# A third group of seven products per pair in the retention's output product

## What is computed

```python
    y = ((y - mu) * lax.rsqrt(var + GN_EPS)).astype(x.dtype)
    y = y.transpose(0, 2, 1, 3).reshape(B, S, H * dv)
    gate = jax.nn.silu(jnp.einsum('bsd,de->bse', x, w_g))
    return jnp.einsum('bse,ed->bsd', gate * y, w_o)
...
        h = layer_norm(DEEPNORM_ALPHA * h + m, ln_g[i, 0], ln_b[i, 0])
```

## Time and profile before

| | |
|---|---|
| median of 3 runs | 2553.68 us (2552.9 to 2553.84) |
| the profiled execution, its own time | 2553.18 us |
| its span, first to last instruction | 2551.4 us |
| PE busy | 2536.5 us (99%) |
| DVE busy | 1809.2 us (71%) |
| ACT busy | 1275.8 us (50%) |
| retention's output product in it | 1655.8 to 1828.6 us |

### The profile page before, as it was taken

How to read it: one execution, slowest core, us unless ns; L and a number is a source line. 1 busy time by engine, 2 the same in 40 slices (tenths; PEclk the granted TensorE clock), 3 DMA queues, 4 the chain that set the end, 5 groups by cost and what they waited for, 6 DMA issues and landing times.

```text
span 2551.4 us, 39946 instructions
## 1 busy us (share of the span) xinstructions
PE 2536.5 (99%) x14214; PEld 2213.2 (87%) x14214; DVE 1809.2 (71%) x2040; ACT 1275.8 (50%) x1427; POOL 15.9 (1%) x39
## 2 busy tenths in 40 slices
PE   9999999999999999999999999999999999999998
PEld 8999888888888888888888888888888888888887
DVE  6666667767676789965655555587866766678997
ACT  4444444555555555534444444454455555555553
POOL 0000000000000000000000000000000000000000
PEclk9999999999999999999999999999999999999999
DMA  8554584555555556655555555546455555556564
GB/s 282 178 172 160 184 256 141 198 196 191 197 192 195 199 212 233 224 176 180 181 176 180 184 179 180 190 182 251 161 191 188 197 197 194 192 198 214 196 228 153
DMA packets 142036, 496.08 MB, mean 194 GB/s; under 512 B 15616, under 2 KB 17920, under 8 KB 141952
## 3 DMA queue, kind: packets, MB, share of 16 engines
q1 hardware_dynamic: 131616, 474.93, 54.2%
q10 hardware_dynamic: 10336, 20.03, 2.5%
HBM read 492.80 MB, written 2.10 MB: 194 GB/s over the span
## 4 chain that ended last, share of the span: by engine, by line
PE 98%; DVE 1%; DMA 1%; issue 0%; ACT 0%; POOL 0%; DVEq 0%; ACTq 0%; SPq 0%; POOLq 0%
PE acc_cm L556 12%; PE acc_ab L556 11%; PE acc_ab L456 9%; PE acc_ab L453 9%; PE acc_ab L455 9%; PE acc_cm L559 6%; PE acc_ab L559 6%; PE acc_ab L467 4%; PE acc_ab L469 4%; PE acc_ab L470 4%; PE acc_cm L453 3%; PE acc_cm L455 3%; PE acc_cm L456 3%; PE acc_cm L725 1%; PE acc_cm L727 1%; PE acc_cm L726 1%
## 5 line engine op out<-in xcount | busy, mean ns | idle before, releaser
L1182 DVE TENSOR_TENSOR w_lo<-raw,w_hi 128x1024 fp32r<-128x1024 f32 x814 | 984.1, 1222 | 536.6 <-ACT w_hi L850 533.1
L850 ACT ACTIVATE w_hi<-raw 128x1024 fp32r<-128x1024 f32 (+1 forms) x818 | 850.6, 1053 | 614.3 <-PE acc_ab L456 181.5
L556 PE MATMUL acc_cm<-x_parts,w_hi 128*128 128x512 f32 x1408 | 480.1, 389 | 0.0
L556 PE MATMUL acc_ab<-x_parts,w_hi 128*128 128x512 f32 x1280 | 436.2, 389 | 0.0
L559 PE MATMUL acc_cm<-x_parts,w_lo 128*128 128x256 f32 x1408 | 388.6, 276 | 0.0
L559 PE MATMUL acc_ab<-x_parts,w_lo 128*128 128x256 f32 x1280 | 353.3, 276 | 0.0
L556 PEld LDWEIGHTS acc_cm<-x_parts,w_hi 128*128 128x128 f32 x1408 | 264.3, 188 | 54.6
L467 PE MATMUL acc_ab<-x_parts,w_hi 128*128 128x256 f32 x1020 | 284.5, 279 | 2.2 <-DVE x_parts L1211 0.9
L556 PEld LDWEIGHTS acc_ab<-x_parts,w_hi 128*128 128x128 f32 x1280 | 240.3, 188 | 49.7
L470 PE MATMUL acc_ab<-x_parts,w_lo 128*128 128x256 f32 x1020 | 281.9, 276 | 0.0
L469 PE MATMUL acc_ab<-x_parts,w_hi 128*128 128x256 f32 x1020 | 281.8, 276 | 0.0
(11 more groups left out here) (214 smaller groups left out, 3618.7 us busy)
## 6 DMA issues: line engine op xcount, KB each, us to landing
raw<-in_weights_dram SPq DMA_DIRECT2D x818, 512.0 KB, 3.8
unit_raw<-in_weights_dram SPq DMA_DIRECT2D x80, 512.0 KB, 8.4
next_raw<-in_weights_dram ACTq DMA_DIRECT2D x12, 512.0 KB, 4.3
ln_gain<-in_ln_g_dram ACTq DMA_DIRECT2D x16, 256.0 KB, 5.4
ln_bias<-in_ln_b_dram ACTq DMA_DIRECT2D x16, 256.0 KB, 7.0
h<-in_x_dram ACTq DMA_DIRECT2D x4, 512.0 KB, 7.7
x_t<-in_x_by_feature_dram SPq DMA_DIRECT2D x7, 256.0 KB, 7.7
raw<-in_weights_dram SPq DMA_DIRECT2D x4, 256.0 KB, 4.7
```

The source lines that it names most:

```text
L556: pe.matmul(acc[:, f], wh[:, k, c], x_parts[:, CK * s + k].rearrange("p a n -> p (a n)"), start=s == 0 and k == 0, stop=False, skip_group_ ...
L850: return act.activation(o, i, ACT.Copy)
L1182: dve.tensor_tensor(wl, raw[:, at % RING], wh.bitcast(F32), ALU.subtract).then_inc(lo_ready, 1)
```

## The change

Stage 1 takes three groups per pair, for heads 0 to 2. Head 2's sums are made in the retention loop as those of heads 0 and 1 are: its pass is written out and the loop over the other heads gets one pass shorter, on ACT and DVE. Six chunks per block are then in groups and ten are plain. So that the number of items is a multiple of four, chunk 11 of the second block is given as two items of one 128-row half each (`HALVED`); a pair has 42 items, the stage 84. The groups stand at items 10, 21, 32, 45, 56 and 66. With three groups per pair the buffers alternate within a pair (`buffer_of`: 0, 1, 0), and a semaphore's count is no longer half the group's number (`unit_use`). The norm's parameters are loaded behind the last group that uses buffer 0 (`SIDE_FREE`): from slot 73, where it was slot 48.

```diff
-UNITS = [4, 2, 4]
+UNITS = [4, 3, 4]
...
-LEAD = [[[12, 16, 20, 24], [4, 8, 12, 16]], [[11, 15], [3, 12]], [[12, 16, 20, 24], [3, 7, 11, 15]]]
-PAIR = [2 * (INNER[g] - 2 * UNITS[g]) + ITEMS * UNITS[g] for g in range(3)]
+LEAD = [[[12, 16, 20, 24], [4, 8, 12, 16]], [[10, 14, 18], [3, 7, 10]], [[12, 16, 20, 24], [3, 7, 11, 15]]]
+
+WHOLE, HALVES = slice(0, CK), [slice(k, k + 1) for k in range(CK)]
+HALVED = [[], [(1, 11)], []]
+PLAIN = [[(b, chunk, part) for b in range(2) for chunk in range(2 * UNITS[g], INNER[g])
+          for part in (HALVES if (b, chunk) in HALVED[g] else [WHOLE])] for g in range(3)]
+PAIR = [len(PLAIN[g]) + ITEMS * UNITS[g] for g in range(3)]
...
+def buffer_of(g, v):
+
+    return v % UNITS[g] % 2
+
+
+def unit_use(g, v):
+
+    return 1 + sum(buffer_of(a, b) == buffer_of(g, v) for a in range(g + 1) for b in range(v if a == g else 2 * UNITS[a]))
...
-              [UNIT_AFTER[g][1] + 5 + s for s in range(RING)] for g in range(3)]
+              [UNIT_AFTER[g][1] + 4 + s for s in range(RING)] for g in range(3)]
+SIDE_FREE = [max(at + ITEMS for v, at in enumerate(UNIT_AT[g]) if buffer_of(g, v) == 0) for g in range(3)]
...
-                            sp.wait_ge(lo_ready, base + unit_at[v - 2] + ITEMS)
+                            before = max(b for b in range(v) if buffer_of(g, b) == buffer_of(g, v))
+                            sp.wait_ge(lo_ready, base + unit_at[before] + ITEMS)
...
-                    return multiply_tile((acc_a, acc_b)[n % 2], t, parts(i % RING, TOKENS), ah, al, CK * chunk, first)
+                    return multiply_tile((acc_a, acc_b)[n % 2], t, [w[:, part] for w in parts(i % RING, TOKENS)], ah, al,
+                                         CK * chunk + part.start, first, count=part.stop - part.start)
...
-                               ln_slots(g + 2, UNIT_AT[g][-2] + ITEMS),
+                               ln_slots(g + 2, SIDE_FREE[g]),
```

More of the change, by code:

```diff
@@ L109, in plain_of @@
 def plain_of(g, i):
-    n, p = divmod(i - ITEMS * sum(at + ITEMS <= i for at in UNIT_AT[g]), INNER[g] - 2 * UNITS[g])
-    return n, 2 * UNITS[g] + p
+    pair, p = divmod(i - ITEMS * sum(at + ITEMS <= i for at in UNIT_AT[g]), len(PLAIN[g]))
+    b, chunk, part = PLAIN[g][p]
+    return 2 * pair + b, chunk, part
+def buffer_of(g, v):
+    return v % UNITS[g] % 2
+def unit_use(g, v):
+    return 1 + sum(buffer_of(a, b) == buffer_of(g, v) for a in range(g + 1) for b in range(v if a == g else 2 * UNITS[a]))
 def skipped(g, i):
@@ L398, in load_turns, with load_unit, load_part @@
                             "a p k n -> p (a k) n")).then_inc(raw_in[s], 16)
-            def load_unit(base, u, at):
+            def load_unit(base, buffer, at):
                 for b in (B11, B21, B12, B22):
-                    sp.dma_start(unit_raw[u % 2][:, b], weights[base + at + b]).then_inc(pair_in[u % 2][b], 16)
+                    sp.dma_start(unit_raw[buffer][:, b], weights[base + at + b]).then_inc(pair_in[buffer][b], 16)
+            def load_part(s, chunk, part):
+                sp.dma_start(raw[:, s, part], weights[chunk, :, part]).then_inc(raw_in[s], 16)
             def load_pairs(g):
@@ L410, in load_pairs @@
                         sp.wait_ge(lo_ready, base + loaded_before(g, i) + 1)
-                        load(i % RING, base + i)
+                        load_part(i % RING, base + i, plain_of(g, i)[2])
                     if i + 1 in unit_at:
@@ L446, in _, with multiply_tile @@
         def _(pe):
-            def multiply_tile(acc, t, weight_parts, xh, xl, kt, first, cols=slice(0, COLS), bank=None):
+            def multiply_tile(acc, t, weight_parts, xh, xl, kt, first, cols=slice(0, COLS), bank=None, count=CK):
                 o = acc[:, t if bank is None else bank, 0:cols.stop - cols.start]
@@ L451, in multiply_tile @@
                 wh, wl = [w[:, :, cols] for w in weight_parts]
-                for k in range(CK):
+                for k in range(count):
                     pe.matmul(o, xh[:, kt + k, c], wh[:, k], start=first and k == 0, stop=False,
@@ L751, in pair_products @@
                     else:
-                        n, chunk = plain_of(g, i)
+                        n, chunk, _ = plain_of(g, i)
                         if n == 0:
@@ L1013, in round_item @@
                     b = (B11, B21, B22)[m]
-                    act.wait_ge(pair_in[v % 2][b], 16 * (one // 2 + 1))
+                    act.wait_ge(pair_in[buffer_of(g, v)][b], 16 * unit_use(g, v))
                 else:
@@ L1044, in pair_stream @@
                         act.wait_ge(raw_in[i % RING], 16 * (Q_PAIRED[g] + i // RING + 1 - skipped(g, i)))
-                        copy(parts(i % RING, TOKENS)[0], raw[:, i % RING]).then_inc(hi_ready, 1)
+                        part = plain_of(g, i)[2]
+                        copy(parts(i % RING, TOKENS)[0][:, part], raw[:, i % RING, part]).then_inc(hi_ready, 1)
                     for step in behind.get(s, ()):
@@ L1182, in split_chunk, with split_part @@
                 dve.tensor_tensor(wl, raw[:, at % RING], wh.bitcast(F32), ALU.subtract).then_inc(lo_ready, 1)
+            def split_part(turn, at, part):
+                dve.wait_ge(hi_ready, RING * turn + at + 1)
+                wh, wl = parts(at % RING, TOKENS)
+                dve.tensor_tensor(wl[:, part], raw[:, at % RING, part], wh[:, part].bitcast(F32),
+                                  ALU.subtract).then_inc(lo_ready, 1)
             def stream(turn, chunks, slots={}, behind={}, place=TOKENS, then=TOKENS, at=0, early_at=None):
```

16 lines of the change are left out of this document (8 added, 8 removed).

## The result

The changed kernel takes 2557.43 us (median of 22 runs, 2556.71 to 2558.19), the kernel before 2553.43 (22 runs, 2552.70 to 2553.93). The ratio is 1.0016, with a 95% interval of 1.0010 to 1.0022: four microseconds slower, and by the bound of 0.2% no difference. 2558.0 was forecast.

A forecast was written before the change was run, and what follows sets the result against it. PE's back-to-back matmuls were taken as the bound, with DVE full beside groups. Terms -2.90 + 0.46 + 4.2 + 1.3 + 1.3 = +4.4 on the median 2553.68 gave 2558.0 us, range 2554.3 to 2562.3.

The forecast's parts named there:

- Removed: Retention's output product on PE: 12 matmuls fewer, -2.72 us; with the last group's 0.18 us of waiting, -2.90.
- Head 2's sums: Retention loop: four sums of head 2, 1 to 2 us, hide in DVE's idle time; cost 0.
- First group: Stage's first group: DVE's ten steps after the last head's low part make item 14's split late, 0.46 us.
- The ledger: The prediction's count of DVE's steps from a fixed point, set against PE's matmul time to the same place.
- Third to fourth group: Six chunks between the pairs' groups: DVE needs 40.92 us, PE 36.72; 4.2 us late, about 1 in the third group.
- End of the stage: Halves just ahead of the last four items: split 83 usable at 8.10, PE wants it at 6.80; 1.3 us late.
- The layer norm's parameters: Layer norm's start: last bias issued 4.9 us after product 77, lands at 11.0, wanted at 9.72; 1.3 us late.
- Rival 1: Groups simply cheaper: DVE keeps up as before and parameters land in time; 2550.8 us, chance 0.10.
- Rival 2: Only the middle: the 4.2 and 0.46 come, the stage's end costs nothing; 2555.5 us, chance 0.12.
- Rival 3: Loads collide at the stage's end: the bias lands 5.3 us late; 2562 us, chance 0.18.
- The rule weighed against the change: Skill's formula prices a DVE addition at 1.224 us; taken as step over 28 instructions, the middle stretch is 2.2 later.
- rival 4: DVE's steps don't overlap: 1.22 us per step for 28 steps; 2560.3 us, chance 0.02.

The follow-up runs named there:

- Run 9: run 8 with separate semaphores for gain and bias loads, each waited for ahead of its first reader: 2550.82 us.
- Run 5: Changed kernel with the stage's token sums rounded, and their low parts written, one product earlier: 2556.71 us.
- run 1: Changed kernel with seven plain chunks instead of six between the third and fourth group: 2556.11 us.
- run 3: Changed kernel with the first pair's four statistics steps moved from between the third and fourth group to behind the fourth: 2555.31 us.
- run 6: Changed kernel with the first three pairs of layer norm parameter loads issued behind the rounding of their slot: 2558.45 us.
- run 10: run 6 with gain and bias loads on separate semaphores, each waited for where it is read: 2556.76 us.
- run 11: Changed kernel with three quarters of this stage's layer norm parameters left out, all eight load issues kept: 2557.12 us.
- Run 7: Changed kernel with the fourth pair of parameter loads issued behind the last slot's two roundings: 2558.20 us.
- run 2: Changed kernel with chunk 7 of the second block given as halves in place of chunk 11: 2558.21 us.
- run 12: run 2 with three quarters of this stage's layer norm parameters left out: 2556.73 us.
- run 4: Changed kernel with groups at items 11, 21, 31, 46, 57, 67, first block's chunk 10 halved, parameters loaded in four consecutive slots: 2552.64 us.
- run 8: run 4 with parameter loads in slots 0, 2, 4, 5 and DVE's wait for them moved behind the last residual sum: 2551.04 us.

## Why the prediction was right, step by step

The forecast of 2558.0 is 0.6 from the median, and the mechanism was the one it named: DVE and not PE sets the pace wherever groups stand close. That the number came so near is in part luck: the layer norm's 1.3 us cost nothing, and small amounts that the sum lacked made up for most of it. By its terms:

- **Removed.** 12 matmuls, as counted. Run 9 shows their value by itself: with nothing late, 2.8 us below the kernel before, where -2.90 was said; in the traces its stage up to the first turning is 2.93 shorter (from the stage's first matmul, 167.58 us in place of 170.51).
- **Head 2's sums, 0.** The low parts of heads 1, 2 and 3 start at 1262.19, 1331.81 and 1401.52 us: the passes take 69.62 and 69.71, before 69.67 and 69.65. Hidden.
- **First group, 0.46.** Measured 0.70. The ledger's ten steps took 11.60 us, not 11.45, because two of the four differences, those that write over the chunk that the split right ahead of them reads, start 1.25 after it (1680.88 to 1682.13 and 1686.68 to 1687.93); the trace of the kernel before has the same step (1745.70 to 1746.94), so "1.13 to 1.15" was read from the other rows. And the matmul behind a wait steps at 0.33, so each wait costs PE 0.1 more than it lasts. Run 5 shows that the low sums are the cause.
- **Third to fourth group, 4.2.** Measured 1.18 + 2.98 = 4.16, split as said. From item 32's split (1721.31) to the fourth group's fifth (1759.64) DVE took 38.33 us, where the ledger's items add up to 38.29. Runs 1 and 3 shift it by the steps of the ledger, from both sides (a chunk more for PE, four steps fewer for DVE). DVE has no idle time in the rows from 1722.58 on: it is busy 12.59 of the fourth group's 12.62.
- **End of the stage, 1.3.** Measured 1.47, in two waits, ahead of items 82 and 83; item 83 starts at 1824.99, 8.19 behind item 77's product, where 8.10 was said. The 1.10 us from the product's end to the rounding were 1.2 (1803.20 + 5 x 2.72 = 1816.80 to 1818.01). With the issues behind the rounding 0.98 of the waits went in run 6 and only 0.26 in run 10, where the chunk came late; run 11 shows that the parameters' traffic is not the cause.
- **The layer norm's parameters, 1.3.** This term was mis-sized; it costs PE nothing: its step into L632 is 0.30 us, before 0.31. The last bias was issued 3.3 us after product 77 (1816.80), and not 4.9. The issues don't stand behind ScalarE's list of roundings, as was reckoned: the first of them comes 0.24 after product 79's end (1819.52), and they run while the rounding at 1819.92 does:

```profile
1819.76 0.33 ACTq L903 DMA_DIRECT2D ln_gain<-in_ln_g_dram  x1
1819.92 1.04 ACT L873 ACTIVATE w_hi<-raw 128x1024 fp32r<-128x1024 f32 x1
1820.12 0.46 ACTq L904 DMA_DIRECT2D ln_bias<-in_ln_b_dram  x1
...
1826.74 0.69 DVE L1356 TENSOR_TENSOR h<-h,acc_ab 128x512 f32<-128x512 f32 x1 [0.66 <-DMA ln_bias<-in_ln_b_dram]
```

  This load landed 6.5 us after its issue, the four biases 5.5 to 7.1, where 6.1 was estimated. But the reason given for 6.1, that the heavy traffic is over by then, was wrong; the windows of the changed kernel have the DMA engines full there (columns as above):

```profile
1815.00:1820.00 5.00, 5.00 (x24) 4.14 (x23) 3.19 (x3) 3.29 (x5) 0.00 (x0) 1.00 0.95 361
1820.00:1825.00 5.00, 4.07 (x18) 2.73 (x16) 5.00 (x6) 3.81 (x5) 0.00 (x0) 1.00 1.02 307
```

  The wait that shows, 0.66, is DVE's, and most of it would have been spent waiting for PE's tile. That there is no slack behind it was right: in run 6 DVE's 3.0 became 2.40 of PE's, and in runs 1, 3 and 5, which reach this place sooner, PE waits 0.18, 0.39 and 0.16 more ahead of L632 than in the changed kernel. Run 7 adds that the landing doesn't follow the issue one for one.
- **Rivals 1 and 2.** The groups were not simply cheaper: DVE's list for the third and the fourth group held within 0.1 us. Rival 2, a stage's end that costs nothing, was right on the parameters, whose issues did run while ScalarE rounded, and wrong on the 1.47.
- **Rival 3, loads that collide.** Not in the changed kernel, but in the variants: 1.0 of run 2's 2.22 us at the end went with the parameters' traffic (run 12), run 4 had ln_bias landings up to 11.6.
- **The rule weighed against the change.** By the formula of the Trainium skill (VectorE: DVE Perf Modes, "The TRN2 errata") an addition of this size is estimated at 1.224 us. Taken as a step, as rival 4 does, that is not what the rows show: from 1752.70 to 1757.37 four steps take 4.67, 1.17 each. The duration of 1.22 agrees with it.

In sum: -2.72, less the 0.11 of waiting that is gone, + 0.7 + 4.16 + 1.47 gives 3.5; the traces differ by 3.73 in the stage. The remaining 0.2 stands in no wait: the steps below 0.29 us add up to 0.19 more than before, among them the second one behind each wait, at 0.23 to 0.24. The medians differ by 4.00, and 4.4 was forecast.

What stays open: how much of the end's 1.47 us the issues are worth by themselves. The landing of the chunk behind them, in time in run 6 and 0.6 late in run 10 with the same order of issues and loads ahead of it, decides that in each execution. The scatter of single executions (0.8 us at the last head's low part) is as large as some of the differences read from one profile each.

## What to carry to other kernels

Fewer products are worth their time only where the engine that prepares them has room: add up that engine's steps from one fixed point to the place in question, and compare with the matmuls' steps up to there. Here the same three groups per pair cost 4 us in one arrangement and gained 2.8 in another. When a wait is taken away, look who was hidden behind it (run 6): put each wait directly ahead of the first reader of what it waits for, and give transfers that are read at different times semaphores of their own.

## What was not expected of the hardware

- The matmul behind a wait steps at 0.33 to 0.34 us in place of 0.227 in nearly all of the waits, so many short waits cost more than their lengths.
- In run 6 PE stood idle from 1829.80 to 1832.04, and the granted clock is 0.50 in the window from 1831.85 to 1835.20 (0.80 and 0.63 in the wider windows above): the lower of the two levels, 1.2 GHz in place of 2.4, which began while PE still waited. Four matmuls in a row stepped at 0.43 us. From the first turning to the next one PE took 3.35 us, in the changed kernel 1.88 (1830.64 to 1832.52): 1.5 us on top of the wait. The waits of up to 1.3 us in the other runs were followed by steps at the full clock.
- An issue of a load on ScalarE mostly takes 0.33 to 0.7 us, but 1.16 (1806.48 in the changed kernel), 1.62 (run 7) and 1.84 (run 8) for the first ln_bias. What is behind it in ScalarE's order waits for it: in the changed kernel the rounding that follows starts at 1807.69, as the issue ends.
